# Weaving four value projections into the head loop of a decoder trunk, with the sample items moved to its end

## Chip, cores and metric

The kernel runs on one NeuronCore of one Trainium2 chip. The time is the device time of one launch in microseconds (us); three runs of the kernel before took 1284.37, 1284.71 and 1288.51 us, median 1284.71.

## The reference, cut to what matters

Two layers work on 512 prompt tokens and 32 sample tokens (8 requests of 4). Layer 0 mixes by causal pooling, layer 1 by differential attention; both also attend to a memory, and both end in an MLP. The change lies in layer 1, where keys and values are projected from the stream and every head's softmaxes are combined:

```
k_new = rope((hk @ w_k).reshape(B, T, 6, 2, 64), pos)
v_new = (hk @ w_v).reshape(B, T, 6, 128)
s = einsum('bqhjd,bkhjd->bhjqk', q, k) * 64 ** -0.5
p = softmax(where(k_pos <= q_pos, s, -1e30))
a = p[:, :, 0] - lam * p[:, :, 1]
o = rmsnorm(einsum('bhqk,bkhe->bqhe', a, v)) * (1 - lam_init)
```

Prompt queries see the prompt's keys. Sample queries see 256 past keys per request, which lie in paged caches in HBM (`cache_k`, `cache_v`, two pages of 128 per request), and their own four.

## The kernel before, in words

Activations lie in SBUF as 8 tiles of 128 features x 544 tokens. A matrix product is cut into 186 **units** of 128 output features: TensorE runs 48 matmuls a unit (8 contraction tiles, three products of a high and a low part, two halves of 272 tokens; `unit`, L415). A unit's weights come by SP's queue into one of four raw slots, ScalarE rounds them to a high part (`high`, L762, the instruction L760), VectorE subtracts for the low part (`rest`, L1024, the instruction L1021), and there are two split slots. So a unit cannot start before the split of its weights, and a split waits for the unit two before it.

In layer 1 the order is: 8 units of w_in with the memory items between them, 6 key units, 6 value units (U_V = 108 to 113), the head loop, 8 units of w_out, the MLP. After each value unit VectorE scales the result into a staging tile (L1339), TensorE turns it (5 transposes, L715 to L718) and ScalarE copies it to `values` (L980, L982). The six key tiles are roped on VectorE, three instructions each (L1346 to L1348), between the value units, after GpSimd's four DMAs have brought the swapped halves (`rotate`, L1424). The queries were roped on GpSimd before (L1495 to L1500).

The **head loop** (`attention`: TensorE L615, ScalarE L851, VectorE L1183) has 28 items. 24 are "diff" items: head a (0 to 5) by query block i (0 to 3), with (i + 1) x 128 keys. Four are "decode" items, for two requests each. `DECODE_AT` gives their places in the list: 8, 12, 17 and 23. An item goes through scores (TensorE, L497; decode L508 and L512), bias (VectorE: mask L1121, maximum L1128, L1132), exp (ScalarE L822), weight (VectorE L1097, L1105, L1107), turn (TensorE transposes L534; decode L537, L539), copy (ScalarE L836), mix (TensorE L572; decode L582), drain (VectorE L1154), clamp (GpSimd L1529) and squares (ScalarE L846, L848). A decode item also needs ScalarE's copy L858 and TensorE's `decode_turn` (L598, matmuls L602), issued two items later; that turn, not the mix, raises `mixed` for a decode item.

TensorE's order in iteration n is scores(n + 2), decode_turn(n - 2) where that is a decode item, turn(n), mix(n - 1). Scores have three slots of two PSUM banks, banks 0 to 5; bank 6 takes the turns and bank 7 the mixes.

**SP's queue** is in order. After the weights of the units up to 115 it calls `load_chunks` (L352) for the four decode items, and only then loads the other weights. A call first waits for `scored` of the decode item before and issues four DMAs of 384 KB for the keys (K), then waits for `mixed` of the decode item before and issues four for the values (V). One set of buffers serves all decode items:

```
                    if at >= 1:
                        sp.wait_ge(used, DEC[at - 1] + 1)
```

where `used` is `scored` for K and `mixed` for V. So for decode items a, b, c in a row, the queue holds K(b), V(b), K(c), V(c), and K(c) stands behind V(b), which waits for decode_turn(a).

`EARLY_DONE` (L308) places the norms of the first four heads in the loop: sums on VectorE, a square root on ScalarE (L865), and four scalings on VectorE (`scale_head`, L1178). After the loop, heads are turned (L727) and split, and the units of w_out begin.

Of the kernel before, what the change touches and what calls it, by code (L numbers as in the profile page):

```python
# [80 lines left out]
DECODE_AT = (8, 12, 17, 23)  # L81
# [21 lines left out]
FIRST_HEAD = 2 * L0_ITEMS  # L103


def build(nc, xT, memT, hist, params, consts, ropes, weights, memK, memV, cacheK, cacheV, pages,
# [5 lines left out]
    with ctx:  # L112
# [16 lines left out]
        def new(name, shape, dt=F32):  # L129
# [18 lines left out]
        memKT = new("mem_keys", [P, 2, MEM_PAIRS, MEM])  # L148
        memVt = new("mem_values", [P, 2, 2, MEM])
# [23 lines left out]
        O = place("attention_out", [P, 24, P], F32, b_at)  # L173
# [4 lines left out]
              [place(f"probs_heads_{s}", [P, 2, 512], F32, b_at + at) for s, at in enumerate((12288, 28672))]]  # L178
        Pr[2].append(T[:, 2:4, :].rearrange("p a b -> p (a b)")[:, 0:1024].rearrange("p (a b) -> p a b", a=2))
# [49 lines left out]
        q_roped, k_roped = sem("q_roped"), sem("k_roped")  # L229
# [64 lines left out]
        def slots(n):  # L294

            return SLOTS if n >= FIRST_HEAD else 2

        def probs(n):
            return Pr[2 if n >= FIRST_HEAD else int(n >= L0_ITEMS)][n % slots(n)]

        def score_banks(n):

            if n < FIRST_HEAD:
                return ps[:, 4:6, :]
            return ps[:, 2 * (n % SLOTS):2 * (n % SLOTS) + 2, :]
# [21 lines left out]
        def _(sp):  # L327
# [24 lines left out]
            def load_chunks(n):  # L352
# [61 lines left out]
        def _(pe):  # L414
# [55 lines left out]
            def scores(n):  # L470
# [3 lines left out]
                if n >= FIRST_HEAD + SLOTS:  # L474
                    pe.wait_ge(exped, n - SLOTS + 1)
                elif n > FIRST_HEAD:
                    pe.wait_ge(exped, FIRST_HEAD)
                elif n:
                    pe.wait_ge(exped, n)
# [14 lines left out]
                elif kind == "diff":  # L494
                    for j in range(2):
# [3 lines left out]
                else:  # L499
                    pe.wait_ge(qbd_ready, 1)  # L500
                    for o in range(2):
                        chunk_ready(pe, k_loaded, chunk_of(n) + o)
# [40 lines left out]
            def mix(n):  # L543
# [26 lines left out]
                elif kind == "diff":  # L570
                    for kt in range(i + 1):
# [33 lines left out]
            def mix_new(n):  # L605
# [3 lines left out]
                for h in range(HEADS):  # L609
                    mm = pe.matmul(ps[:, 2 * ((n - 1) % SLOTS), SAMPLE * h:SAMPLE * (h + 1)]  # L610
# [3 lines left out]

            def attention(n0, n1):  # L615

                for n in range(n0, n1):
                    if n + 2 < n1:
# [79 lines left out]
            for j in range(MIXT + 1):  # L698
                if j < MIXT:
                    unit(U_V + j, j, B)  # L700
                if j >= 1:
                    h = j - 1
                    if h == MIXT - 1:
                        pe.wait_ge(q_roped, 1)
                        pe.wait_ge(k_roped, 1)
                        pe.wait_ge(v_ready, h)
                        pe.wait_ge(unit_out, U_V + h)
                        scores(FIRST_HEAD)
                        scores(FIRST_HEAD + 1)
                    pe.wait_ge(unit_out, U_V + h + 1)  # L710
                    if h == 0:
                        pe.wait_ge(drained, FIRST_HEAD)
                    if h >= 2:
                        pe.wait_ge(v_ready, h - 1)
                    for t in range(QT):  # L715
                        pe.transpose(ps[:, 4 + 2 * (h % 2), lo_of(t)], T[:, h % TS, lo_of(t)], ident)
                    pe.transpose(ps[0:SAMPLE, 5 + 2 * (h % 2), 0:P], T[:, h % TS, PROMPT:TOK], ident)\
# [940 lines left out]
```

## Time and profile before

| what | value |
|---|---|
| median of three runs | 1284.71 us |
| profiled execution | 1290.19 us, span 1288.2 us |
| TensorE busy | 1220.3 us (95%) |
| VectorE / ScalarE / GpSimd busy | 584.3 / 409.1 / 356.7 us |
| key and value units and head loop | within 645 to 821 us of the span |

The profile names engines PE (TensorE matmuls), PEld (its weight loads), DVE (VectorE), ACT (ScalarE), POOL (GpSimd) and SPq (SyncE's DMA issues). Starts are us from the span's start. "idle before" is how long the engine stood still before an instruction and what ended it. PEclk is TensorE's granted clock as a share of full speed.

### The profile page before, as it was taken

How to read it: one execution, taken by the hardware profiler on the slowest of the kernel's cores; microseconds unless marked ns; L12 is line 12 of the kernel's file. 1: busy time of each engine (PE TensorE's matmuls, PEld its weight loads, DVE VectorE, ACT ScalarE, POOL GpSimd, SP SyncE). 2: the span in 40 equal slices, each digit the busy share in tenths (PEclk: the TensorE clock that was granted, in tenths of full speed). 3: DMA queues.
4: the chain of work that ended last, by engine and by line, in shares of the span. 5: the costliest groups of instructions: out<-in, count | busy, mean ns of one | idle time of the engine just before them, and what ended most of it. 6: DMA issues, size and time to landing. Idle time of an engine off the chain costs nothing.

```text
span 1288.2 us, 23147 instructions
## 1 busy us (share of the span) xinstructions
PE 1220.3 (95%) x9556; PEld 1169.2 (91%) x9556; DVE 584.3 (45%) x867; ACT 409.1 (32%) x754; POOL 356.7 (28%) x290
## 2 busy tenths in 40 slices
PE   6998999999999999999999888699999999999994
PEld 5877999999999999998799655699999999999994
DVE  7676444333333333446635867545333333333334
ACT  6544342212212112334412456433211211211221
POOL 3363024205205205320062200013402512502524
PEclk9999999999999999999999889599999999999997
DMA  7623422232322332232344546023222323222211
GB/s 277 210 85 107 124 97 82 84 97 82 85 97 82 88 94 82 83 90 80 135 128 119 202 149 212 1 66 95 86 82 85 96 83 90 91 85 88 90 50 70
DMA packets 37056, 132.97 MB, mean 103 GB/s; under 512 B 4226, under 2 KB 5122, under 8 KB 36322
## 3 DMA queue, kind: packets, MB, share of 16 engines
q1 hardware_dynamic: 35858, 123.42, 30.6%
q0 software_dynamic: 1104, 8.15, 2.2%
q8 instruction: 76, 1.25, 0.4%
q14 instruction: 18, 0.15, 0.0%
HBM read 121.18 MB, written 7.03 MB: 100 GB/s over the span
## 4 chain that ended last, share of the span: by engine, by line
PE 88%; DVE 7%; ACT 2%; issue 1%; DMA 0%; DVEq 0%; POOL 0%; SPq 0%; ACTq 0%
PE psum L432 81%; DVE inv_rms L1040 1%; DVE weights_split L1021 1%; PE psum L572 1%; PE psum L483 1%; ACT weights_split L760 1%; PE psum L497 1%; DVE tiny L1128 1%; PE psum L534 1%; PE psum L508 1%; PE psum L554 1%; PE psum L528 0%; PE psum L582 0%; PE psum L512 0%; DVE probs_heads L1107 0%
## 5 line engine op out<-in xcount | busy, mean ns | idle before, releaser
L432 PE MATMUL psum<-operand_b,weights_split 128*128 128x272 f32 x4416 | 562.6, 289 | 3.9 <-DVE weights_split L1021 3.7
L432 PEld LDWEIGHTS psum<-operand_b,weights_split 128*128 128x128 f32 x4416 | 556.7, 189 | 8.8 <-DVE weights_split L1021 4.7
L432 PE MATMUL psum<-operand_a,weights_split 128*128 128x272 f32 (+1 forms) x4116 | 529.7, 291 | 23.4 <-DVE weights_split L1021 18.3
L432 PEld LDWEIGHTS psum<-operand_a,weights_split 128*128 128x128 f32 x4116 | 523.4, 191 | 29.1 <-issue 21.9
L760 ACT ACTIVATE weights_split<-weights_raw 128x1024 fp32r<-128x1024 f32 (+1 forms) x186 | 192.6, 1035 | 392.1 <-PE psum L432 392.1
L1021 DVE TENSOR_TENSOR weights_split<-weights_raw,weights_split 128x1024 fp32r<-128x1024 f32 (+1 forms) x186 | 239.8, 1289 | 135.3 <-ACT weights_split L760 135.2
L1412 POOL TENSOR_TENSOR squares<-staging 128x544 f32<-128x544 f32 x64 | 76.3, 1193 | 469.8 <-ACT operand_a L806 207.6
L1075 DVE TENSOR_TENSOR residual<-psum,residual 128x544 f32<-128x544 f32 x48 | 34.8, 725 | 175.9 <-PE psum L432 175.9
L1056 DVE SCALAR_TENSOR_TENSOR staging<-psum,inv_rms 128x544 f32<-128x544 f32 x56 | 40.6, 725 | 150.1 <-PE psum L432 150.1
L1405 POOL TENSOR_TENSOR squares_sum<-squares_sum,squares 128x544 f32<-128x544 f32 (+1 forms) x35 | 48.6, 1388 | 115.7 <-ACT squares L772 115.1
L1414 POOL TENSOR_TENSOR operand_a<-squares,operand_a 128x544 fp32r<-128x544 f32 x32 | 65.0, 2030 | 2.5
L1414 POOL TENSOR_TENSOR operand_b<-squares,operand_b 128x544 fp32r<-128x544 f32 x32 | 64.9, 2027 | 2.5
L1044 DVE TENSOR_TENSOR residual<-psum,residual 128x544 f32<-128x544 f32 x32 | 23.2, 725 | 64.1 <-PE psum L432 64.1
L806 ACT ACTIVATE operand_a<-staging 128x544 fp32r<-128x544 f32 x24 | 15.8, 659 | 109.9 <-DVE staging L1056 109.9
L806 ACT ACTIVATE operand_b<-staging 128x544 fp32r<-128x544 f32 x24 | 15.8, 658 | 109.8 <-DVE staging L1056 109.8
L772 ACT ACTIVATE squares<-residual 128x544 f32<-128x544 f32 x40 | 25.8, 646 | 36.3 <-DVE residual L1044 36.3
L1128 DVE TENSOR_REDUCE tiny<-psum 128x2 f32<-128x512 f32 (+3 forms) x40 | 30.8, 770 | 9.8 <-PE psum L483 8.9
L1405 POOL TENSOR_TENSOR squares_sum<-squares 128x544 f32<-128x544 f32 (+1 forms) x6 | 8.2, 1364 | 88.6 <-ACT squares L772 88.6
L767 ACT ACTIVATE operand_a<-residual,params 128x544 fp32r<-128x544 f32 x16 | 12.0, 751 | 64.0 <-DVE residual L1044 64.0
L1529 POOL TENSOR_SCALAR squares<-attention_out 128x128 f32<-128x128 f32 x24 | 7.0, 293 | 87.2 <-DVE attention_out L1154 87.2
L836 ACT ACTIVATE staging<-psum 128x512 f32<-128x512 f32 (+4 forms) x48 | 22.4, 467 | 26.4 <-PE psum L534 22.4
L767 ACT ACTIVATE operand_b<-residual,params 128x544 fp32r<-128x544 f32 x24 | 17.8, 741 | 37.7 <-DVE residual L1044 37.7
(201 smaller groups left out, 720.3 us busy)
## 6 DMA issues: line engine op xcount, KB each, us to landing
weights_raw<-in_weights SPq DMA_DIRECT2D x180, 512.0 KB, 3.6
cache_tiles<-in_page_k SPq DMA_DIRECT2D x16, 384.0 KB, 3.8
cache_tiles<-in_page_v SPq DMA_DIRECT2D x16, 384.0 KB, 4.0
cache_tiles<-in_mem_k SPq DMA_DIRECT2D x8, 512.0 KB, 4.7
cache_tiles<-in_mem_v SPq DMA_DIRECT2D x8, 512.0 KB, 5.9
residual<-in_x SPq DMA_DIRECT2D x1, 2176.0 KB, 11.7
out_y<-projected SPq DMA_DIRECT2D x8, 272.0 KB, 2.1
rotated<-projected POOLq DMA_DIRECT2D x4, 408.0 KB, 7.1
```

The lines of the kernel that those rows point to most:

```text
L432: mm = pe.matmul(ps[:, 2 * (j % PS) + hf, 0:n], w(wr), act[:, ar, k, hf * n:(hf + 1) * n], start=(q == 0 and wr == 0 and ar == 0), stop=(q ...
L760: act.activation(split[:, s % HL, 0, 0:n], raw[:, s, 0:n], ACT.Copy).then_inc(weight_hi, 1)
L767: act.activation(dst, src, ACT.Copy, scale=gain(g, k)).then_inc(norm_hi, 1)
L772: act.activation(SQ[:, k % 2, 0:cols], src, ACT.Square).then_inc(sq_ready, 1)
L806: act.activation(hidden[:, 0, j, :], T[:, j % TS, :], ACT.Square).then_inc(hid_hi, 1)
L1021: dve.tensor_tensor(split[:, s % HL, 1, 0:n], raw[:, s, 0:n], split[:, s % HL, 0, 0:n].bitcast(F32), ALU.subtract).then_inc(weight_lo, 1)
L1056: dve.scalar_tensor_tensor(out=halves(T[:, j % TS, :]), in0=unit_psum(j), scalar=0.0, in1=halves(rms[:, :]), op0=ALU.max, op1=ALU.mult).th ...
L1075: dve.tensor_tensor(halves(X[:, j, :]), unit_psum(j), halves(X[:, j, :]), ALU.add)\
L1128: own.chain(dve.tensor_reduce(mx[:, s, :], sc[:, :, 0:n_keys], AX.X, ALU.max))
L1405: pool.tensor_tensor(sq_sum[:, 0:cols], a, SQ[:, k % 2, 0:cols], ALU.add).then_inc(sq_summed, 1)
L1412: pool.tensor_tensor(sq, t, t, ALU.mult).then_inc(hid_sq, 1)
L1414: pool.tensor_tensor(hidden[:, 1, j, :], sq, hidden[:, 0, j, :].bitcast(F32), ALU.subtract)\
```

## The change

Four value projections go into the head loop. Units 108 and 109 run as before it, with the turn of the first in the middle of the second; unit 110 is cut into thirds of its contraction tiles, with the first two items' scores between them. In each of the loop's first 13 iterations (PIECES) TensorE ends with one **piece**: the turn of a value tile, or a third of units 111, 112 and 113. These units use banks 0 and 1, so until item 16 (THREE_FROM) scores have two slots, and TensorE's order is turn(n), scores(n + 2), mix(n - 1), piece; from iteration 14 (ONE_AHEAD) it is as before. Key tile 0 is still roped on VectorE, tiles 1 to 5 on GpSimd, with a semaphore count of their own. The decode items move to places 17, 20, 22 and 25. The first squares come six items late instead of three, and four at once in iteration 14. Buffers move: the attention output lies in two regions, and the probabilities of two slots where the memory keys and values were. `load_chunks` gets one more wait (for GpSimd's roping) and is otherwise as it was.

```diff
-DECODE_AT = (8, 12, 17, 23)
+DECODE_AT = (17, 20, 22, 25)
...
+V_EARLY = 2
+THIRDS = ((0, 1, 2), (3, 4, 5), (6, 7))
+PIECES = 4 * (MIXT - V_EARLY) - 3
+THREE_FROM = FIRST_HEAD + PIECES + 3
+ONE_AHEAD = THREE_FROM - 2
...
                 if n == DEC[4]:
                     sp.wait_ge(k_roped, 1)
+                    sp.wait_ge(k_roped_late, HEADS - 1)
...
+                if n == THREE_FROM:
+                    pe.wait_ge(v_ready, MIXT)
+                elif n >= FIRST_HEAD + 2:
+                    pe.wait_ge(exped, slot_before(n) + 1)
...
+            def value_third(j, part):
+                if part == 0:
+                    pe.wait_ge(weight_lo, U_V + j + 1)
+                    if j == V_EARLY:
+                        pe.wait_ge(unit_out, U_V + 1)
+                    else:
+                        pe.wait_ge(v_ready, j)
+                for k in THIRDS[part]:
+                    for wr, ar in ((0, 0), (0, 1), (1, 0)):
+                        for hf in range(2):
+                            mm = pe.matmul(ps[:, hf, 0:HALF], split[:, j % HL, wr, lo_of(k)],
...
+            def value_piece(q):
+                if q % 4 == 0:
+                    value_turn(V_EARLY + q // 4, 0)
+                else:
+                    value_third(V_EARLY + 1 + q // 4, q % 4 - 1)
...
                 for n in range(n0, n1):
-                    if n + 2 < n1:
+                    if n >= ONE_AHEAD and n + 2 < n1:
                         scores(n + 2)
                     if n - 2 in DECODE:
                         decode_turn(n - 2)
                     turn(n)
+                    if n < ONE_AHEAD:
+                        scores(n + 2)
                     if n > n0:
                         mix(n - 1)
+                    if n - n0 < PIECES:
+                        value_piece(n - n0)
...
+            unit(U_V, 0, B)
+            unit(U_V + 1, 1, B, mid=first_turn)
+            value_third(2, 0)
+            pe.wait_ge(q_roped, 1)
+            scores(FIRST_HEAD)
+            value_third(2, 1)
+            pe.wait_ge(v_ready, 1)
+            value_turn(1, 6)
+            scores(FIRST_HEAD + 1)
+            value_third(2, 2)
...
 # ScalarE, in iteration n, after items_exp(n + 1)
+                    if 1 <= n - n0 <= PIECES and (n - n0) % 4 == 1:
+                        value_copy(V_EARLY + (n - n0) // 4, 0)
...
+                    if n - n0 < PIECES and (n - n0) % 4 == 0:
+                        high(U_V + V_EARLY + (n - n0) // 4 + HL)
...
 # VectorE, iterations before ONE_AHEAD
+                    if filling:
+                        value_out(j)
+                    items_weight(n + 1)
+                    items_bias(n + 2)
+                    if n > n0:
+                        items_drain(n - 1)
+                    if filling:
+                        rest(U_V + j + HL)
...
 # GpSimd
+            pool.wait_ge(k_swapped, 64)
+            for h in range(1, HEADS):
+                own.step(pool.tensor_tensor(swap[:, h, :], swap[:, h, :], rope[:, 1, :], ALU.mult))
+                own.chain(pool.tensor_tensor(Kt[:, h, :], Kt[:, h, :], rope[:, 0, :], ALU.mult))
+                pool.tensor_tensor(Kt[:, h, :], Kt[:, h, :], swap[:, h, :], ALU.add).then_inc(k_roped_late, 1)
```

## Rows read from the trace of the kernel before

**Rows 1.** The page's busy times and its clock row in 40 slices.
```profile
PE 1220.3 (95%) x9556; PEld 1169.2 (91%) x9556; DVE 584.3 (45%) x867; ACT 409.1 (32%) x754; POOL 356.7 (28%) x290
...
PEclk9999999999999999999999889599999999999997
```

**Rows 2.** Busy us by stage: window, length, PE, PEld, DVE, ACT, POOL, clock, DMA, GB/s.
```profile
681.30:719.50 38.20, 38.20 (x310) 38.15 (x309) 24.50 (x31) 9.88 (x15) 2.94 (x5) 1.00 0.35 88
719.50:725.70 6.20, 3.25 (x25) 1.80 (x23) 5.10 (x13) 4.01 (x13) 5.24 (x13) 1.00 0.61 186
725.70:749.00 23.30, 19.63 (x116) 13.34 (x116) 19.35 (x55) 14.46 (x58) 3.65 (x10) 0.78 0.75 275
...
804.40:821.10 16.70, 11.12 (x52) 9.11 (x48) 9.16 (x28) 9.15 (x38) 0.88 (x3) 0.68 0.00 0
821.10:832.40 11.30, 7.14 (x29) 6.04 (x29) 8.58 (x23) 7.42 (x16) 0.29 (x1) 0.50 0.00 0
832.40:840.00 7.60, 7.60 (x42) 7.60 (x43) 1.86 (x3) 0.00 (x0) 0.00 (x0) 0.65 0.01 2
```

**Rows 3.** TensorE in order of time, a value unit, its turn, the loop's first turn.
```profile
713.40 6.25 PE L432 MATMUL psum<-operand_b,weights_split 128*128 128x272 f32 x48
719.49 0.60 PE L716 MATMUL psum<-constants,staging 128*128 128x128 f32 x4
...
725.68 0.33 PE L534 MATMUL psum<-constants,staging 128*128 128x128 f32 x1 [0.62 <-DVE staging L1107]
```

**Rows 4.** VectorE in order of time: key tile 0 waits for the swapped halves.
```profile
695.70 0.72 DVE L1346 TENSOR_TENSOR rotated<-rotated,cos_sin 128x544 f32<-128x544 f32 x1 [5.88 <-DMA rotated<-keys]
```

**Rows 5.** TensorE in order of time: parts of items at full clock.
```profile
735.75 0.92 PE L497 MATMUL psum<-keys,projected 64*128 64x384 f32 x4
736.59 0.33 PE L534 MATMUL psum<-constants,probs_heads 128*128 128x128 f32 x1
...
740.04 1.92 PE L508 MATMUL psum<-cache_tiles,query_blocks 128*32 128x256 f32 x24
741.89 1.52 PE L512 MATMUL psum<-keys,query_blocks 128*128 128x32 f32 x12
...
749.88 1.16 PE L572 MATMUL psum<-values,staging 128*128 128x128 f32 x8
...
752.08 1.50 PE L582 MATMUL psum<-cache_tiles,staging 128*32 128x384 f32 x16
...
756.59 0.53 PE L602 MATMUL psum<-constants,staging 128*128 128x128 f32 x3
```

**Rows 6.** SP's queue in order of time: first issue, length of the four issues.
```profile
744.18 3.64 SPq L373 DMA_DIRECT2D cache_tiles<-in_page_k  x4
757.87 3.69 SPq L373 DMA_DIRECT2D cache_tiles<-in_page_v  x4
762.67 3.65 SPq L373 DMA_DIRECT2D cache_tiles<-in_page_k  x4
```

**Rows 7.** DMA issues of 762 to 767 us: KB, us to landing.
```profile
cache_tiles<-in_page_k SPq DMA_DIRECT2D x4, 384.0 KB, 4.4
```

**Rows 8.** Windows of one us behind that load, columns as in rows 2.
```profile
769.00:770.00 1.00, 1.00 (x10) 0.28 (x4) 0.00 (x0) 0.56 (x3) 0.00 (x0) 0.79 0.41 163
770.00:771.00 1.00, 1.00 (x8) 0.44 (x6) 0.00 (x0) 0.36 (x1) 0.00 (x0) 1.00 0.02 9
```

**Rows 9.** What SP's queue waited for, 655 to 833 us: total, times, longest.
```profile
SPq L371 <- PE psum L602: 21.8, 3, 9.3
```

**Rows 10.** GpSimd in order of time, while it ropes the queries.
```profile
659.48 2.34 POOL L1497 TENSOR_TENSOR projected<-projected,cos_sin 128x544 f32<-128x544 f32 x1
```

**Rows 11.** VectorE's split in the same stretch and a later one.
```profile
664.54 2.42 DVE L1021 TENSOR_TENSOR weights_split<-weights_raw,weights_split 128x1024 fp32r<-128x1024 f32 x1 [0.43 <-ACT weights_split L760]
...
698.37 1.22 DVE L1021 TENSOR_TENSOR weights_split<-weights_raw,weights_split 128x1024 fp32r<-128x1024 f32 x1
```

**Rows 12.** TensorE in order of time: the new keys' mix at the loop's end.
```profile
816.30 2.77 PE L610 MATMUL psum<-probs_new,values_new 32*128 32x32 f32 x12
```

More of the change, by code:

```diff
@@ L147, in build @@
         k_at = take(4 * HEADS * TOK)
-        memKT = new("mem_keys", [P, 2, MEM_PAIRS, MEM])
-        memVt = new("mem_values", [P, 2, 2, MEM])
+        memk_at, memv_at = take(16 * MEM), take(16 * MEM)
+        memKT = place("mem_keys", [P, 2, MEM_PAIRS, MEM], F32, memk_at)
+        memVt = place("mem_values", [P, 2, 2, MEM], F32, memv_at)
         QbdM = new("mem_query_blocks", [P, REQS, MEM_PAIRS, 32])
@@ L697, in _, with first_turn @@
                 unit(U_K + j, j, B, ready=normed(G_KV) if j == 0 else None)
[L698 to L717, printed above, removed]
-                        .then_inc(v_turned, 1)
-            pe.wait_ge(unit_out, U_OUT1)
-            pe.wait_ge(v_ready, MIXT)
+            def first_turn():
+                pe.wait_ge(drained, FIRST_HEAD)
+                value_turn(0, 6)
+            unit(U_V, 0, B)
[8 more added lines that the diff above has]
+            value_third(2, 2)
+            pe.wait_ge(v_ready, 2)
             attention(FIRST_HEAD, len(ITEMS))
@@ L1179, in scale_head, with value_out @@
                 rows = slice(QT * h, QT * h + QT)
-                dve.tensor_tensor(O[:, rows, :], O[:, rows, :], rr2[:, rows].unsqueeze(2).to_broadcast([P, QT, P]),
+                dve.tensor_tensor(O_rows(rows.start, rows.stop), O_rows(rows.start, rows.stop), rr2[:, rows].unsqueeze(2).to_broadcast([P, QT, P]),
                                   ALU.mult).then_inc(sub_scaled, 1)
-            def attention(n0, n1):
-                items_bias(n0)
-                items_bias(n0 + 1)
-                for n in range(n0, n1 + 2):
-                    if n < n1:
+            def value_out(j):
+                dve.wait_ge(unit_done, U_V + j + 1)
+                if j >= 2:
+                    dve.wait_ge(v_turned, j - 1)
+                at = unit_psum(j) if j < V_EARLY else ps[:, 0:2, 0:HALF]
+                dve.tensor_tensor(halves(T[:, 2 + j % 2, :]), at, halves(rms[:, :]), ALU.mult).then_inc(unit_out, 1)
+            def attention(n0, n1):
+                for n in range(n0, ONE_AHEAD):
+                    filling = n - n0 < PIECES and (n - n0) % 4 == 0
+                    j = V_EARLY + (n - n0) // 4
+                    if filling:
[6 more added lines that the diff above has]
+                        rest(U_V + j + HL)
+                for n in range(ONE_AHEAD, n1 + 2):
+                    if ONE_AHEAD < n < n1:
                         items_weight(n)
-                    if n - 2 >= n0:
+                    if n > ONE_AHEAD:
                         items_drain(n - 2)
@@ L1334, in _ @@
                 rest(U_K + j + HL)
[L1335 to L1354 removed]
+            value_out(0)
+            rest(U_V + HL)
+            dve.wait_ge(cat_hi, 2)
+            dve.tensor_tensor(A[:, 1, 6:8, :], Z[:, 6:8, :], A[:, 0, 6:8, :].bitcast(F32), ALU.subtract)\
+               .then_inc(cat_lo, 1)
+            dve.wait_ge(k_swapped, 64)
+            own.step(dve.tensor_tensor(swap[:, 0, :], swap[:, 0, :], rope[:, 1, :], ALU.mult))
+            own.chain(dve.tensor_tensor(Kt[:, 0, :], Kt[:, 0, :], rope[:, 0, :], ALU.mult))
+            dve.tensor_tensor(Kt[:, 0, :], Kt[:, 0, :], swap[:, 0, :], ALU.add).then_inc(k_roped, 1)
+            value_out(1)
+            items_bias(FIRST_HEAD)
+            rest(U_V + 1 + HL)
+            items_bias(FIRST_HEAD + 1)
+            items_weight(FIRST_HEAD)
             attention(FIRST_HEAD, len(ITEMS))
```

152 lines of the change are left out of this document (82 added, 70 removed).

## The prediction

> **What bounds the kernel now.** The page's busy times come first: TensorE is busy for 95% of the span, no other engine for half of it, and the clock row holds 9 almost everywhere except in the slices that cover about 708 to 837 us [rows 1]. So time is to be had only where TensorE stands still or is slow, and the views by stage show where. The value units (681.3 to 719.5 us) are full at clock 1.00. The 6.2 us behind them, the fill of the head loop, hold 3.25 us of TensorE work. The loop's first stretch gives 19.63 us of work in 23.3 us at a mean clock of 0.78. Its last 16.7 us run at 0.68, and from 821.1 us to about 837 us the clock is at the lower of its two levels, 1.2 GHz [rows 2]. The loop is a chain through three engines: in the first stretch VectorE is busy for 19.35 of 23.3 us [rows 2], some 2.6 us for a diff item, against some 1.85 us of TensorE work for one at full clock (worked out below). That is the room which the value units are to fill. A value unit takes 6.0 us from its start to its turn's, the turn 0.44 us, and the loop's first turn comes at 725.68 us [rows 3].
>
> **Part 1, the start.** Units 108 and 109 and a turn end at 681.3 + 12.0 + 0.44 = 693.8 us [rows 2, 3]. A third of 18 matmuls is 18/48 of 6.0 = 2.25 us, so TensorE asks for the first scores at 696.0. Key tile 0 isn't roped by then: its swapped halves land at 695.70, after which VectorE needs three instructions of 0.72 [rows 4], to 697.8. The wait is 1.9 us; nothing else is queued that could use it. Then come scores 0.45, third 2.25, turn 0.44, scores 0.5, the last 12 matmuls 1.5: 703.2. ScalarE reaches the first exp only behind the copy of value tile 1 (turned at 701.2), so the first turn comes at about 704.1, 21.6 us before its present place.
>
> **Part 2, three cycles of four items.** A diff item with i = 0 to 3 costs TensorE, start to start at full clock, scores 0.45, 0.5, 0.85, 1.05; turn 0.25, 0.4, 0.65, 0.9; mix 0.2, 0.4, 0.75, 1.0. The three rows of such parts that stand here [rows 5] give 0.92, 0.33 and 1.16 as durations, which overlap their neighbours by some 0.1. Four items are 7.4 us, with a unit and its turn 13.85. VectorE has four items at 2.6, the scaling 0.72 and the split 1.22: 12.4 us, so it isn't the bound. Only the first third waits: it needs the value copy, which ScalarE does behind the exp of two items on; following the instructions through gives 1.0 to 1.3 us a cycle, 15.1 us in all. Item 12's turn comes at 704.1 + 3 x 15.1 = 749.4 us.
>
> **Part 3, to the first decode turn.** From there to the end of decode_turn(17) in iteration 19 the order holds 21.0 us of TensorE work: seven diff items' parts, a value turn, twice the decode scores (1.85 + 1.45), a decode turn of 0.85, a decode mix 1.45, its late turn 0.4 [rows 5]. Waits add 1.0 us for the last value copy (item 16 takes back banks 0 and 1) and 2.0 us for K(20), which is free to load at scored(17), only three short iterations ahead: it needs 7.2 to 7.5 us by rows (1.0 to the first issue, 3.3 to the last, the rest landing) [rows 6, 7] against 5.5 us of work. 773.7 us.
>
> **Part 4, the loads, the term that decides.** K(22) stands in SP's queue behind V(20), and V(20) waits for decode_turn(17). Before, that order costs nothing: K(17) is asked for five iterations after decode_turn(8), and SP, not TensorE, is the one that waits, three times and 21.8 us in all [rows 9]. Its length can be read: the decode turn begins at 756.59 and takes 0.53 [rows 5], V's first issue follows at 757.87, K's first at 762.67, its last 3.3 us later [rows 6], and it lands about 3.7 us after that; DMA activity ends between 769 and 770 us [rows 8]. That is 12.6 us from turn to landing. In the new order scores(22) is the first thing in iteration 20, and only turn(19) and mix(18), 1.05 us, lie between. TensorE stands for 11.5 us, to 786.3, with turn(20) and everything after queued behind the wait on its in-order queue; VectorE and ScalarE run dry as well. The same again with decode_turn(20) and K(25): 1.85 us of work lie between, so 10.7 us. A third, smaller one: V(25) waits for decode_turn(22) and lands 0.75 + 3.3 + 3.9 = 8.0 us later, when some 4.5 us of work are left to do.
>
> The Trainium skill (DMA: Bandwidth & Descriptors, Anatomy of one DMA) has a fixed 2.0 us and the bytes at 436 GB/s, 2.9 us for 384 KB; here four such issues took a median of 4.4 us [rows 7]. By the page each chain would be about 1 us shorter and the sum 3 us less; I take the rows.
>
> **Clock after a stand.** No row shows a stand of 11 us. The nearest: after 821.1 to 832.4 us with 7.14 us of work, TensorE stays at half clock though full from 832.4, and the mean of 0.65 up to 840.0 says that the lower level lasts for 0.70 x 7.6 = 5.3 us of it [rows 2]. So scores(22) and scores(25), 3.3 us each, take 5.9 (5.2 at half clock, 0.7 at full). Ends: 3.3 us each, 6.6 us each.
>
> **The sum.** 773.7 + 12.6 (K(22)) + 5.9 (its scores) + 5.8 (turn 20, mix 19, scores 23, turn 21, mix 20, scores 24, decode_turn(20), with ScalarE's copy) + 12.6 (K(25)) + 5.9 + 3.0 (to decode_turn(22)) + 8.0 (V(25)) + 8.5 (mix 25, its late turn, turn 27, mix 26, the new keys' mix, mix 27: 6.4 at full clock, 10.5 where all of it is at half, as the new keys' mix of 2.77 is now [rows 12]) = 836.0 us. The loop ends now at 821.1 [rows 2], so it is 14.9 us later. What stands behind it is unchanged and already at half clock [rows 2]: nothing. Costed at nothing too: the late squares (four at once, some 3 us of ScalarE, under the wait of iteration 14 and 15), the first heads' norms (2.6 us of table loads and 2.5 us of scaling now hold TensorE near 806 us; they fall into the first stand), GpSimd's stores, the moved buffers. The profiled execution had 1290.19 us, 5.5 above the median of 1284.71; its own forecast is 1305, that of the median 1284.7 + 14.9 = 1299.5.
>
> **Rivals.** (1) *The lock costs more.* While GpSimd ropes, its 1.36 us instructions take up to 2.34 [rows 10], and VectorE's split takes 2.42 instead of 1.22 [rows 11]. In the new order GpSimd ropes five tiles from 698 to about 720 us, beside five weight steps and two splits of VectorE. Some 0.7 us each, 5 us, if TensorE's pieces don't cover it: 1304.5. The Trainium skill (SBUF — State Buffer, SBUF: two separate sides) has the shared port pair as a lock for the whole instruction, against a VectorE instruction with two SBUF inputs. The trace agrees. For covering it speaks that VectorE has 2.7 us of slack in a cycle. Chance 0.17. (2) *The other side: the loads land in time.* If K(22) and K(25) were there when asked for, the stands of 11.5 and 10.7 us, 3.5 at V(25) and the 5.2 us of slow clock go, the loop ends near 805, and the kernel takes 1269. It decides at whether SP issues K(22) at least 12.6 us before iteration 20; the one queue order speaks against. It also covers an error of mine in it. Chance 0.08. (3) *The stands are there, but the rest is quicker:* full clock after them (7.3 us less) and parts 1 to 3 without half their 7 us of waits: 1288, about even. Chance 0.07. The forecast has 0.68.
>
> **Numbers.** Forecast 1299.5. With full clock after the stands it is 1292, with waits missing in parts 1 to 3 another 4 less, 1288; with half clock to the end 2 more, with the lock 5 more, 1307. Two in ten lie outside, mostly rival 2. About 0.3%, 4 us, is what a measurement can tell from no change. Faster 0.09, within 0.06, slower 0.85.
>
> **What would show it.** Right: TensorE idle for 10 to 12 us ahead of two runs of L508-like decode scores, released by DMA of cache_tiles, about 12.6 us after a decode turn, half clock behind them; cycles of about 15 us at clock 1.00 from 704 to 749; first turn near 704. Wrong: no idle above 5 us ahead of decode scores; cycles of 18 us or more with TensorE waiting for VectorE; the loop's end before 821.

## The result, and the profile after

The changed kernel takes 1329.22 us (1323.97 to 1333.79, 4 runs) beside 1286.61 for the kernel before in the same comparison, a ratio of 1.0323 [1.03, 1.0346]. The profiled execution took 1330.01 us, its span 1328.1. Slower, as forecast, but by 42.6 us where the forecast had 14.8; the time lies 22 us above 1307, the upper end of the range.

The page's busy times and clock row of the changed kernel, which answer to [rows 1]:
```profile
PE 1225.8 (92%) x9556; PEld 1169.5 (88%) x9556; DVE 580.8 (44%) x852; ACT 408.4 (31%) x754; POOL 382.5 (29%) x305
...
PEclk9999999999999999999998976789999999999997
```
TensorE has 5.5 us more busy time and the span is 39.9 us longer, so most of the loss is standing still. What TensorE waited for in the changed kernel (total us, times, longest); line numbers are those of the changed kernel, where L536 and L611 are the decode items' scores and mix, L523 the diff scores, L655 the value units' thirds:
```profile
PE psum L536 <- DMA cache_tiles<-in_page_k: 26.7, 3, 11.9
...
PE psum L655 <- ACT values_new L918: 4.4, 3, 2.6
...
PE psum L536 <- issue: 3.8, 1, 3.8
PE psum L523 <- DVE keys L1427: 3.7, 1, 3.7
...
PE psum L611 <- DMA cache_tiles<-in_page_v: 2.5, 1, 2.5
```
The kernel before has no wait of TensorE on a cache tile. "issue" means that the profile names no releaser. Busy time of the changed kernel by stage, columns as in [rows 2]: start to first turn, three cycles to item 12's turn, to the end of decode_turn(17), of decode_turn(20), of decode_turn(22), to the loop's end, to the first unit of the output weights:
```profile
691.00:711.10 20.10, 14.33 (x92) 13.17 (x91) 11.79 (x16) 4.26 (x13) 14.52 (x10) 0.83 0.33 87
711.10:757.50 46.40, 41.95 (x289) 34.19 (x290) 37.88 (x89) 25.12 (x91) 12.34 (x15) 0.96 0.28 105
757.50:793.10 35.60, 25.63 (x173) 15.51 (x172) 17.96 (x50) 17.71 (x80) 9.25 (x24) 0.81 0.26 92
793.10:820.80 27.70, 15.42 (x87) 9.59 (x84) 9.91 (x36) 8.56 (x26) 0.59 (x2) 0.63 0.35 115
820.80:844.50 23.70, 12.39 (x76) 7.28 (x76) 4.50 (x20) 3.23 (x14) 0.29 (x1) 0.64 0.40 133
844.50:861.90 17.40, 11.49 (x71) 6.87 (x69) 7.84 (x30) 7.46 (x30) 0.88 (x3) 0.80 0.62 212
861.90:872.50 10.60, 4.16 (x29) 3.28 (x29) 8.58 (x23) 7.27 (x16) 0.29 (x1) 0.89 0.00 1
```
The woven stretch is as full as was meant (41.95 of 46.40 us). Of the next three stages, 87 us in all, TensorE works 53.4 us, and at clocks of 0.81, 0.63 and 0.64. The first unit of the output weights starts at 872.5 instead of 832.4 us [rows 2]: 40.1 us later, which is the whole difference of the spans. TensorE in order of time at the decode scores of items 17, 20, 22 and 25 and at V(25) (in brackets the idle time before and its releaser):
```profile
770.47 3.63 PE L536 MATMUL psum<-cache_tiles,query_blocks 128*32 128x256 f32 x24 [3.81 <-issue]
...
784.85 3.60 PE L536 MATMUL psum<-cache_tiles,query_blocks 128*32 128x256 f32 x24 [3.71 <-DMA cache_tiles<-in_page_k]
...
806.41 3.63 PE L536 MATMUL psum<-cache_tiles,query_blocks 128*32 128x256 f32 x24 [11.94 <-DMA cache_tiles<-in_page_k]
...
834.14 3.63 PE L536 MATMUL psum<-cache_tiles,query_blocks 128*32 128x256 f32 x24 [11.03 <-DMA cache_tiles<-in_page_k]
...
853.85 2.79 PE L611 MATMUL psum<-cache_tiles,staging 128*32 128x384 f32 x16 [2.50 <-DMA cache_tiles<-in_page_v]
```
All four runs of scores take 3.6 us where [rows 5] has 1.92: the lower clock. SP's queue of the changed kernel shows the chain:
```profile
777.19 3.64 SPq L396 DMA_DIRECT2D cache_tiles<-in_page_k  x4
793.87 3.67 SPq L396 DMA_DIRECT2D cache_tiles<-in_page_v  x4
798.65 3.65 SPq L396 DMA_DIRECT2D cache_tiles<-in_page_k  x4
821.57 3.63 SPq L396 DMA_DIRECT2D cache_tiles<-in_page_v  x4
825.97 3.63 SPq L396 DMA_DIRECT2D cache_tiles<-in_page_k  x4
```
V(20) is issued 0.8 us after decode_turn(17) ends (793.1), K(22) behind it at 798.65, and the scores start at 806.41, 13.3 us after the turn.

### The profile page after: what moved, and what is told of

Read it like the earlier page. It is cut to its first block, busy times and chain, and to the rows that moved or that the text cites. A ratio compares the mean times of both kernels' runs of the same rounds, so it can differ in the third digit from the quotient of the medians.

```text
span 1328.1 us, 23173 instructions
## 1 busy us (share of the span) xinstructions
PE 1225.8 (92%) x9556; PEld 1169.5 (88%) x9556; DVE 580.8 (44%) x852; ACT 408.4 (31%) x754; POOL 382.5 (29%) x305
## 3 DMA queue, kind: packets, MB, share of 16 engines
q1 hardware_dynamic: 35858, 123.42, 29.7%
## 4 chain that ended last, share of the span: by engine, by line
PE 85%; DVE 6%; DMA 3%; ACT 2%; issue 2%; SPq 2%; POOL 0%; DVEq 0%; ACTq 0%; POOLq 0%
PE psum L455 76%; PE psum L655 2%; DVE inv_rms L1107 1%; DVE weights_split L1088 1%; PE psum L536 1%; DMA cache_tiles<-in_page_k 1%; DMA rotated<-keys 1%; SPq L394 1%; PE psum L506 1%; ACT weights_split L816 1%; PE psum L601 1%; PE psum L611 1%; PE psum L540 1%; SPq L396 1%; PE psum L523 1%
## 5 line engine op out<-in xcount | busy, mean ns | idle before, releaser
L455 PEld LDWEIGHTS psum<-operand_b,weights_split 128*128 128x128 f32 x4224 | 532.5, 189 | 8.8 <-DVE weights_split L1088 4.7
L1492 POOL TENSOR_TENSOR operand_a<-squares,operand_a 128x544 fp32r<-128x544 f32 x32 | 64.9, 2029 | 2.5
L1492 POOL TENSOR_TENSOR operand_b<-squares,operand_b 128x544 fp32r<-128x544 f32 x32 | 64.9, 2027 | 2.5
L536 PE MATMUL psum<-cache_tiles,query_blocks 128*32 128x256 f32 x96 | 14.5, 632 | 30.5 <-DMA cache_tiles<-in_page_k 26.7
L536 PEld LDWEIGHTS psum<-cache_tiles,query_blocks 128*32 128x32 f32 x96 | 6.2, 164 | 36.1 <-issue 36.1
L655 PE MATMUL psum<-operand_b,weights_split 128*128 128x272 f32 x192 | 30.2, 315 | 4.4 <-ACT values_new L918 4.4
L898 ACT ACTIVATE staging<-psum 128x512 f32<-128x512 f32 (+4 forms) x48 | 22.3, 465 | 36.5 <-PE psum L562 32.5
```

The lines of the kernel that those rows point to most:

```text
L455: mm = pe.matmul(ps[:, 2 * (j % PS) + hf, 0:n], w(wr), act[:, ar, k, hf * n:(hf + 1) * n], start=(q == 0 and wr == 0 and ar == 0), stop=(q ...
L536: pe.matmul(sc[row:row + 32, 0, 0:PAST].rearrange("p (g k) -> p g k", g=PAGES), Qbd[:, h, 2 * a + o, 32 * g:32 * g + 32], keys[:, h, :, :] ...
L655: mm = pe.matmul(ps[:, hf, 0:HALF], split[:, j % HL, wr, lo_of(k)], B[:, ar, k, hf * HALF:(hf + 1) * HALF], start=(k == 0 and wr == 0 and ...
L1492: pool.tensor_tensor(hidden[:, 1, j, :], sq, hidden[:, 0, j, :].bitcast(F32), ALU.subtract)\
```

## The experiments

Each comparison has its own runs of the kernel before, with medians of 1284.9 to 1286.6 us. The ratios are to it, with their 95% intervals. A ratio can differ from the quotient of the medians by some 0.2% (experiments 11 and 16), so 2 us between two versions decide nothing.

**1. The order of the loads.** The changed kernel, with each key tile issued ahead of the value tile of the item before it.
```
-            for n in DEC[4:]:
-                load_chunks(n)
+            for n, part in ((4, 0), (4, 1), (5, 0), (6, 0), (5, 1), (7, 0), (6, 1), (7, 1)):
+                load_chunks(DEC[n], (part,))
```


> The changed kernel with SP's calls for the decode items in another order: K(22) goes ahead of V(20), and K(25) ahead of V(22); nothing else is changed. Theory (the queue order makes the two long stands): K(22) is then released by scored(20), which ends at 789.9 us of the span, and lands about 8.5 us later, near 798.5 instead of 806.4, so TensorE's stand ahead of scores(22) falls from 11.9 to about 4 us; K(25) is released by scored(22), nearly 10 us of other work ahead of its use, and its stand of 11.0 us goes. With the half clock behind it the kernel gains 18 to 24 us: 1305 to 1311. Rival A (the loads are limited by their own transfer, or by the other traffic, not by the place in the queue): the stands stay above 9 us each and the time within 5 us of 1329. Rival B (the port and the query blocks carry most of the loss, and other waits take the stands' place): both stands shrink but the time falls by less than 8 us.


Measured 1308.38 us, 1.0174 [1.0133, 1.0214]: 20.8 us back, as the theory had it. The waits of this version (its lines are 2 further down):
```profile
PE psum L538 <- DMA cache_tiles<-in_page_k: 4.9, 2, 3.8
PE psum L613 <- DMA cache_tiles<-in_page_v: 4.3, 2, 2.3
```
The stands of 11.9 and 11.0 us came from the queue's order, not from the transfers' length.

**2 and 3. The two smaller stands.** The query blocks two items earlier, and GpSimd's roping behind VectorE's first tile:
```
-                    if n - FIRST_HEAD == PIECES - 4:
+                    if n - FIRST_HEAD == PIECES - 6:
```


> The changed kernel with GpSimd's query blocks two items earlier in its order (behind the clamp of item 7 instead of item 9). Theory (scores(17) waits for them: they end at 770.4 us, and TensorE stands 1.6 and 3.8 us until 770.5): they start when value unit 113 is done, near 757.7, and end near 764, the stand of 3.8 us goes, and the half clock around 765 to 773 with it: 5 to 8 us less, 1321 to 1324. The two stands of 11 to 12 us stay as they are. Rival (ScalarE's late squares are what holds the items there: with the clamps of items 8 and 9 later, the four squares of iteration 14 come later and hold the exp): the time changes by less than 2 us, with TensorE waiting for weights of items 14 to 16 instead.


```
             pool.wait_ge(k_swapped, 64)
+            pool.wait_ge(k_roped, 1)
```


> The changed kernel with GpSimd starting on key tiles 1 to 5 only when VectorE has roped tile 0. Theory (the two engines hold each other up where both rope at once: VectorE's second and third instruction took 1.85 and 1.73 us instead of 0.72): tile 0 is ready 2.3 us sooner, TensorE's stand ahead of the first scores falls from 3.7 to about 1.5 us, the third and turn behind it don't fall to half clock, and the kernel gains 3 to 6 us, 1323 to 1326. GpSimd's tiles end 2 us later, which nothing waits for. Rival (the long instructions have another cause, or what is gained is lost at the next wait, the value copy of item 1): VectorE's instructions stay at 1.7 to 1.9 us, or the time stays within 2 us of 1329.


Measured 1327.4 us, 1.032 [1.0273, 1.0367], and 1326.41 us, 1.0298 [1.0255, 1.0341]: gains of 1.8 and 2.8 us, less than the runs scatter and less than either theory had, so the trace must say what they are. In the first the stand of 3.81 is gone, and item 12's turn to the end of decode_turn(17) takes 31.7 instead of 35.6 us. But the scores of item 17 still take 3.63: the half clock was not that stand's. It begins before it, in the changed kernel too, where the mix ahead of the stand already takes 1.20 us instead of 0.71:
```profile
765.47 1.20 PE L601 MATMUL psum<-values,staging 128*128 128x128 f32 x4 [1.55 <-issue]
```
 In the second experiment VectorE ropes its tile at the old price again; this is VectorE in order of time, first the changed kernel, then the one with the wait:
```profile
696.94 1.85 DVE L1426 TENSOR_TENSOR keys<-keys,cos_sin 128x544 f32<-128x544 f32 x1
698.83 1.73 DVE L1427 TENSOR_TENSOR keys<-keys,rotated 128x544 f32<-128x544 f32 x1
```
```profile
698.65 0.72 DVE L1426 TENSOR_TENSOR keys<-keys,cos_sin 128x544 f32<-128x544 f32 x1
699.41 0.72 DVE L1427 TENSOR_TENSOR keys<-keys,rotated 128x544 f32<-128x544 f32 x1
```
TensorE's wait on it falls from 3.74 to 1.77 us, the start from 20.1 to 17.0. The third behind the wait still runs at half clock (4.05 us, and 2.42 for the third ahead of it), which the theory had excluded, and the first cycle takes 18.2 us instead of 16.8. The changed kernel's own start also varies: it takes 18.4, 18.8 and 18.8 us in experiments 1, 2 and 13, which leave it as it is. At item 12's turn, 64.8 us after the first value turn, experiment 3 is no further than those three (64.9 to 65.4; 66.5 in the changed kernel). So the cause of the long instructions is shown, a gain in time is not.

**4. The places alone.** The kernel before, with one line of the change:
```
-DECODE_AT = (8, 12, 17, 23)
+DECODE_AT = (17, 20, 22, 25)
```


> The kernel before with one line changed: the decode items at places 17, 20, 22 and 25 instead of 8, 12, 17 and 23; no value work is woven in, and keys are roped on VectorE as before. Theory (the close places make the stands, whatever else is in the loop): two stands of 10 to 12 us ahead of scores(22) and scores(25), some 2 to 4 us ahead of scores(20), 2 to 3 us at V(25), half clock behind them: 26 to 34 us more than before, 1313 to 1320. Rival (the stands need the woven loop, which uses up the work that covered the loads): less than 8 us more, stands below 4 us. It also gives what the rest of the change is worth: the changed kernel's 1329 less this one's time.


Measured 1325.19 us, 1.0291 [1.0238, 1.0343]. Its waits name the same stands:
```profile
PE psum L508 <- DMA cache_tiles<-in_page_k: 25.2, 3, 11.7
```
This line alone costs 39 us, 5 more than the theory's upper end. Everything else in the change adds 4 to it, within the scatter of the two; the expectation of 1313 to 1320 had left 9 to 16 us for it.

**5 and 6. All three mendings, and the places with the mended queue.**


> The changed kernel with three edits together: K(22) and K(25) ahead of V(20) and V(22) in SP's queue, the query blocks two items earlier, and GpSimd's roping behind VectorE's. Theory (three waits that add up on one path): against the changed kernel's 1329.2 us the first gave 20.8 us; in the traces the second took 3.9 us off the stretch from item 12's turn to decode_turn(17) and the third 2 to 3 us off the start. Together 1301 to 1305, still 15 us or more above the kernel before, because four decode items within nine places leave stands of 2 to 4 us at K(20), K(22) and V. Rival (they hide each other: what one gives, the next wait takes back): 1306 to 1310, as with the first alone.

> The kernel before with the decode items at 17, 20, 22 and 25 and K(22), K(25) ahead of V(20), V(22) in SP's queue. Theory (the stands come from the places and the queue alone): the new queue order gives what it gave the changed kernel, 18 to 24 us: 1301 to 1307, stands of about 4 us ahead of scores(22) and none ahead of scores(25). With the runs so far this closes a square of woven or not by queue order, and the woven work is worth 0 +- 5 us in both rows. Rival (the two interact: the woven loop shifts work ahead of the loads): a gain below 12 us or above 28.


Measured 1303.44 us, 1.0137 [1.0101, 1.0173], and 1306.94 us, 1.0154 [1.011, 1.0199]. With woven units the places cost 1329.2, with the mended queue 1308.4; without them 1325.2 and 1306.9: the queue's order is worth some 20 us in both, and weaving is worth nothing in either. Both times lie where the theories had them. In the three-edit version a new stand of 6.68 us appeared at K(20). The DMA issues of 768 to 783 us there (KB, us to landing):
```profile
out_v_prompt<-values POOLq DMA_DIRECT2D x1, 1536.0 KB, 7.4
cache_tiles<-in_page_k SPq DMA_DIRECT2D x4, 384.0 KB, 7.3
```

**7 to 9. The store, and places three items apart.** The three-edit version with decode items at 16, 19, 22, 25 (7), with the store of the values three items earlier (8), and with both (9):
```
-                    if n - FIRST_HEAD == PIECES - 1:
+                    if n - FIRST_HEAD == PIECES - 4:
                         pool.wait_ge(v_ready, MIXT)
```


> The three edits of the run before on the changed kernel, and the decode items at 16, 19, 22 and 25, three places apart. Theory (what is left of the stands follows from the distance between decode items): K(22) gets a third iteration of cover, its stand of 3.8 us falls below 1.5, V's stands of 2.0 and 2.3 us fall by half; against that, scores(16) is asked for one iteration sooner and stands 1 to 3 us for the query blocks. Net 1 to 5 us less than the run with the three edits: 1298 to 1303. Rival (VectorE's pace, not the loads, holds the second half of the loop): within 1 us of that run, the waits named for VectorE's weights instead of DMA.

> The three-edit version of the changed kernel (1303.4 us), and GpSimd's stores of the prompt's values moved from the last score item but one to four before the end, so that they are no longer in the DMA rings together with the key tile of item 20. Theory (the store stretched that tile's landing to 11.6 us after its issue): its stand shrinks from 6.7 to 2 to 3 us and the time comes to 1298 to 1301 us. Rival (the tile is late by its own chain, the store only happened to stand beside it): the stand stays at 5 us or more, the time at 1302 to 1306 us.

> The version with the stores moved as well, with decode items at 16, 19, 22 and 25. If the store was what gave item 19's key tile its stand of 6.9 us in the earlier spread by three, the stand falls to under 3 us and the time to 1296 to 1301 us. If places by three gain nothing by themselves, it stays within 2 us of the version with the stores moved and the old places.


Measured 1304.28 us, 1.0143 [1.0115, 1.0172]; 1300.28 us, 1.0106 [1.0067, 1.0146]; 1302.79 us, 1.0113 [1.0071, 1.0156]. Only the eighth came out as its theory had it; the seventh and the ninth took longer than theirs. The seventh kept the collision (6.94 us at K(19)). With the store moved, K(20) stands 3.12 us, and the same view, which here holds six issues of two loads, has
```profile
cache_tiles<-in_page_k SPq DMA_DIRECT2D x6, 384.0 KB, 3.7
```
so the store was what stretched the landing. By the medians that is worth some 3 us, though the two intervals overlap. Three apart instead of two gains nothing: in the ninth the key stands are down to 2.3 us in all, but the query blocks (2.9 us), VectorE's combining (4.0 us) and the late turns (3.8 us) hold TensorE instead.

**10 and 11. The kernel before with spread places,** 13, 17, 21, 25, without and with keys first.


> The kernel before with the decode items at 13, 17, 21 and 25: late, but four places apart. Theory (the distance decides: a K load stands behind a turn that comes two iterations after the decode item before the last, and needs 13.3 us; with places a, b, c there are c - a - 4 iterations for it, one in the changed kernel, four here at some 3.3 us each): no stand above 1 us ahead of any scores, and 1283 to 1291 us, as before. Rival (it is the lateness that costs: the first items without decode work run at VectorE's pace with TensorE partly idle and slow, and the decode work comes on top at the end): 1295 us or more, without DMA stands.

> The kernel before with decode items at 13, 17, 21 and 25 (1295.1 us alone) and the key load of the next item issued ahead of the value load. Theory A (what the spread places still cost, about 10 us, is the two key stands of 3.1 and 2.6 us and the half clock behind them): no stand of TensorE on a key tile over 1 us, time 1284 to 1290 us. Theory B (a decode item that lies late costs by itself, whatever its loads do): no key stand either, but the time stays at 1292 us or more.


Measured 1295.11 us, 1.0088 [1.0061, 1.0115], and 1298.4 us, 1.0079 [1.0051, 1.0107]. The first theory failed: key tiles still let TensorE stand for 3.10 and 2.62 us, and the four iterations that the theory counted did not cover the load. The time is the rival's, but the rival had no such stands. The second expectation's theory A failed by its time. But its trace doesn't bear out B either. TensorE's waits there:
```profile
PE psum L584 <- DMA cache_tiles<-in_page_v: 7.5, 3, 4.8
```
The key stands are gone and a value tile, now behind the key tile in the queue, stands 4.8 us in their place. Whether lateness costs by itself this pair could not say.

**12. Another stand of the kernel before,** tried as a version that might beat both: EARLY_HEADS = 3 instead of 4.


> The kernel before with three instead of two of the closing step's head groups treated ahead of the last decode item, so that the norms of that group lie beside busy TensorE work instead of at 802 to 808 us, where TensorE stands 2.6, 0.5 and 2.5 us and then runs 26 us at a lower clock. Theory: these stands go and the clock stays up, 1276 to 1283 us. Rival (another wait at the end of the loop takes their place, or the extra scaling delays it): within 0.3% of before, 1283 to 1290 us.


Measured 1291.82 us, 1.0042 [1.0024, 1.0059]: slower by 0.4%, outside what theory and rival had. The loop then norms three heads instead of four, and does so earlier. The clock at 811 to 821 us rose to 0.83 from 0.50, but stands of 2.98 us (a late turn, 789.9), 2.29 (815.4) and 1.88 (828.3) took the place of those removed, and the output weights start at 833.9 instead of 832.4.

**13 to 16. No late loads at all.** What was open: whether late places cost anything but waiting for tiles. The loads of the last three decode items are left out (those items compute their part from the first one's tiles again), in the changed kernel (13) and in the kernel before with places 13, 17, 21, 25 (14), its own (15), and 17, 20, 22, 25 (16):
```
-            for n in DEC[4:]:
-                load_chunks(n)
+            load_chunks(DEC[4])
...
-            eng.wait_ge(loaded[n % 2], done)
+            eng.wait_ge(loaded[n % 2], min(done, 96))
```


> The changed kernel without the key and value loads of its last three decode items (they read again the tiles of item 17, so that part of the samples' attention to the cache is computed from other pages). Theory A (all that the places cost is waiting for loads, with the half clock behind it): no stand of TensorE on a cache tile, and 1286 to 1294 us. Theory B (a late place costs 10 us or more by itself, whatever its loads do): no stand either, but 1298 to 1310 us.

> The kernel before with decode items at 13, 17, 21 and 25, without the loads of the last three (they read the first one's tiles again). Theory A: 1283 to 1289 us, as before. Theory B: 1292 us or more.

> The kernel before with its own places, without the loads of the last three decode items (they read the first one's tiles again). Both theories: its trace shows no stand of TensorE on a cache tile, so 1283 to 1288 us. If it gains more than 4 us, the loads cost something there too that the list of waits does not name, and the other three runs are read against this one.

> The kernel before with decode items at 17, 20, 22 and 25, without the loads of the last three. Theory A: 1284 to 1292 us. Theory B: 1296 us or more. Against the changed kernel without the same loads it says what the woven projections are worth when no load is in their way: by the forecast's sum for the first half they should be 8 us or more ahead, by the runs so far about nothing.

| version | us | ratio | with the loads |
|---|---|---|---|
| 13 changed | 1290.26 | 1.0023 [1.0002, 1.0044] | 1329.2 |
| 14 before, spread | 1283.75 | 0.9979 [0.9961, 0.9997] | 1295.1 |
| 15 before | 1285.63 | 1.0 [0.9979, 1.002] | 1286.3 |
| 16 before, late | 1287.4 | 0.9989 [0.9971, 1.0008] | 1325.2 |

Theory A holds in all four. In the kernel before the loads cost nothing, in the late places 38 to 39 us, and a late place costs at most some 2 us by itself. Woven (13) against not woven (16), the projections are 2.9 us behind by the medians even when no load is in the way.

These two show why. The starts of the diff turns of items 0, 4, 8 and 12 in version 16:
```profile
728.35 0.33 PE L533 MATMUL psum<-constants,staging 128*128 128x128 f32 x1 [0.62 <-DVE staging L1106]
...
738.35 0.33 PE L533 MATMUL psum<-constants,probs_heads 128*128 128x128 f32 x1
...
750.49 0.47 PE L533 MATMUL psum<-constants,probs_heads 128*128 128x128 f32 x1
...
761.56 0.33 PE L533 MATMUL psum<-constants,staging 128*128 128x128 f32 x1
```
and in version 13:
```profile
708.42 0.30 PE L561 MATMUL psum<-constants,probs_heads 128*128 128x128 f32 x1 [1.60 <-issue]
...
725.34 0.27 PE L561 MATMUL psum<-constants,probs_heads 128*128 128x128 f32 x1
...
740.14 0.27 PE L561 MATMUL psum<-constants,probs_heads 128*128 128x128 f32 x1
...
754.96 0.27 PE L561 MATMUL psum<-constants,probs_heads 128*128 128x128 f32 x1
```
Both are counted from VectorE's read of value unit 108 (690.09 and 686.81), up to which the two kernels have done the same work; the first value turn would not do, as the woven kernel runs it half a unit earlier. The first diff turn comes after 38.3 us unwoven and 21.6 woven, 16.7 ahead. Twelve items then take 33.2 us unwoven and 46.5 woven, 13.3 more for three units and turns of 6.4 us: of 19.3 us, 6.0 are hidden. Item 12's turn is at 71.5 and at 68.2 us: the woven kernel leads by 3.3. Up to the end of decode_turn(17) it then loses 8.3 us (30.3 against 22.0), with the 3.8 us stand before the scores of item 17 and their half clock among them, and up to the output weights it regains 3.1. In all it takes 142.2 us against 140.4.

## Why the forecast was right in direction and wrong in size

The direction was right, and for the reason given: the queue's order makes the two long stands. The size was wrong by the terms below. These are the steps against the changed kernel's profile, in us:

| end of | forecast | measured | late by |
|---|---|---|---|
| part 1, first turn | 704.1 | 711.1 | 7.0 |
| part 2, item 12's turn | 749.4 | 757.5 | 8.1 |
| part 3, decode_turn(17) | 773.7 | 793.1 | 19.4 |
| decode_turn(20) | 798.0 | 820.8 | 22.8 |
| decode_turn(22) | 819.5 | 844.5 | 25.0 |
| loop | 836.0 | 861.9 | 25.9 |

The last step is 25.9 us late. The medians miss by 29.7 (1329.2 for 1299.5), chiefly because the profiled run of the kernel before lay 5.5 us above its median and that of the changed kernel 0.8.

**Part 4, the mechanism: right, the clock behind the stands: too short.** The forecast's K(22) chain of 12.6 us measured 13.3, its stand 11.94 for 11.5, K(25)'s 11.03 for 10.7; the chain of V(25) took 9.3 for 8.0. Reordering the queue took the longer stand down to 3.8 us and removed the other (experiment 1), doing the places alone made them (4). This part is 6.5 us short: 0.7, 0.7 and 1.3 in the chains, 0.5 in the scores (6.1 for 5.9 each), and 2.5 and 1.3 in the short iterations up to decode_turn(20) and decode_turn(22) (8.3 for 5.8, 4.3 for 3.0), less 0.5 at the end. The short iterations are late by the clock. The forecast took from the stretch at 832 us [rows 2] that TensorE is back at full clock after 5.3 us of work. Behind K(22) it works without a gap from 806.41 on, and this is its busy time and clock (columns as in [rows 2]):
```profile
810.00:815.00 5.00, 5.00 (x24) 4.63 (x23) 1.92 (x6) 0.87 (x3) 0.00 (x0) 0.50 0.00 0
815.00:820.00 5.00, 5.00 (x32) 2.47 (x30) 3.78 (x10) 4.96 (x15) 0.29 (x1) 0.60 0.01 3
```
So the lower level lasts until 819.0, for 12.6 us of work. Behind K(25) it lasts for 8.8 us.

**Part 3: the largest failed step, 11.3 us.** GpSimd's query blocks, which every decode item's scores read, were not in the sum. The change moves them: before, GpSimd makes them ahead of all clamps (L1506, L1511), now behind the clamp of item 9 (L1595, L1600), which the section on the change doesn't list. TensorE stood 3.81 us for them, because each of the clamps ahead of them waits for ScalarE's late squares. The profile names no releaser for this stand, but the blocks end at 770.38 and the scores start at 770.47, and with the blocks earlier the stand is gone (experiment 2). GpSimd in order of time in the changed kernel:
```profile
763.77 0.29 POOL L1613 TENSOR_SCALAR squares<-attention_out 128x128 f32<-128x128 f32 x1 [3.51 <-ACT squares L910]
764.12 2.66 POOL L1595 MEMSET query_blocks<- 128x3072 f32 x1
766.85 3.53 POOL L1600 COPY query_blocks<-projected 64x32 f32<-64x32 f32 x12
```
The forecast costed the squares at nothing under other waits, and did not ask who waits for them. Besides this stand there were another (1.55 us before a mix, ahead of this one), half clock in two runs of decode scores that had been priced at full clock (3.63 + 1.80 and 3.60 + 1.52 for 1.85 + 1.45 each: 2.1 and 1.8 us), and K(20), 3.7 for 2.0. That makes 11.0 of the 11.3. (749.4 and the 24.0 us of this part also make 773.4, not 773.7.) The half clock was costed only behind the long stands. Here it came without one: it was there before the 3.81 us stand, after stands of 0.85 and 1.55, and again behind the 3.71 us at K(20).

**Part 1: the second failed step, 7.0 us.** The wait for key tile 0 was 3.74 us, not 1.9: VectorE's two last instructions on it take 1.85 and 1.73 us beside GpSimd's 1.86 and 1.80. That is rival 1's mechanism (the lock), at a place the rival did not name, ahead of all weaving. The stand brings half clock: the third behind it takes 4.45 us, the one ahead of it 2.42. Of the 7.0 us, 1.0 lies ahead of the wait, 1.8 is the wait, 3.1 is the half clock behind it, and 1.1 a longer stand before the first turn (2.04 for 0.9). The Trainium skill (SBUF — State Buffer, SBUF: two separate sides) has the shared port pair locked for a whole instruction; the trace agrees here, 1.85 against 0.72, and so does experiment 3, where the two no longer overlap and VectorE takes 0.72 again.

**Part 2: right within 1.1 us.** Cycles of 16.8, 14.8 and 14.8 us for 15.1 each, clock 0.96. The first is long by a stand of 2.55 us and the half clock of the third behind it (3.77 us).

**The clock over all parts.** Busy time times one less the clock, stage by stage in the rows above, gives an estimate of what half clock cost up to the loop's end: some 21 us. The forecast had 7.3 (2.6 each behind K(22) and K(25), 2.1 at the end). So about 14 of the 25.9 us are half clock that it left out, in every part, and the rest is standing still.

**The rivals.** Rival 2 priced the kernel with its loads in time at 1269; version 13 has 1290.3. So the loads are worth 39 us where forecast less rival had 30.5, and 21 us of the miss lie outside them. Of these 21 the profile of version 13 shows some 13, up to the output weights: item 12's turn is 5.6 us late, and part 3, without K(20), takes 30.3 us for 22.3. The rest is again the profiled runs against their medians. The room for the woven work was read nearly right: the forecast's own numbers, 15.1 us a woven cycle against four items at 2.6, leave 1.7 of 6.4 us hidden, and 2.0 were. But the forecast never set the two side by side, and so it did not say how small the gain of the weaving is next to what it costed at nothing. Rival 3 (full clock behind the stands) was wrong in each case. GpSimd's stores, costed at nothing, cost some 3 us once the stands before them were mended (experiment 8); in the change itself no run tells them apart. The Trainium skill's figure for one load, which the forecast set beside its rows (DMA: Bandwidth & Descriptors, Anatomy of one DMA), is there that of a DMA issued by GpSimd, and these are SP's; the measured chains were longer than the rows, not shorter.

The range failed for the same reason: its ends, 1288 and 1307, varied the clock behind two stands, half of the waits in parts 1 to 3 and the lock, and held no term for what had been costed at nothing.

No version with all its loads beat the kernel before. The best with woven units is at 1300.3, the best with late places and unwoven units at 1295.1. With no late loads at all the spread places give 1283.75, 0.2% less than the kernel before, so at the places tried here better buffering has some 0.2% to win (0.4% by the interval). A second buffer for the key tiles wasn't tried.

## What to carry to other kernels

Before an item is moved, follow its loads in the issuing queue, not only in memory: a load behind another load that waits for a consumer inherits the consumer's chain, here 13.3 us from turn to data, and the items between must cover that. Ask the same of every small helper costed at nothing: which engine makes it, what stands ahead of it in that engine's order, and whether those wait. And price an interleaving as the woven stretch less the unwoven one, cycle for cycle; leaving out a suspected transfer altogether is a direct way to see how much of a loss is waiting for it.

## What the runs showed of the hardware

- Half clock can follow a short stand of TensorE as well as a long one, and the length of the last stand alone does not decide it. The scores of decode items took 1.92 us behind stands of 0.71, 1.17, 2.17 and 2.62 us (experiments 7, 1, 2, 10), but 3.21 to 3.38 behind stands of 0.68, 1.60, 2.87 and 2.88 (9, 9, 9, 7), and 3.2 to 3.63 behind each of those of 3.0 us or more. They can be at half clock without a stand just before them (experiment 2, 3.63).
- The lower level then lasted for 12.6 and 8.8 us of gapless work behind the stands of 11.94 and 11.03 us.
- An elementwise instruction of VectorE and one of GpSimd on key tiles at the same time took 1.85 and 1.86 us, where VectorE alone takes 0.72 and GpSimd alone 1.35.
- With a 1.5 MB store of GpSimd's queue issued half a microsecond earlier, 384 KB loads took 7.3 us to land (experiment 5); with the store moved away they took 3.7 (experiment 8).
- Profiles of one kernel differ in this stretch by more than its medians do: from the first value turn to the output weights the kernel before takes 139.1 us, the same kernel without loads it never waits for 133.3, while their medians are 0.7 us apart. The profiled executions differ as much in their whole time (1290.19 and 1284.48 us). Comparisons of a few microseconds need the medians and the stage windows both.
